# Two attentions of a second transformer block: both heads of a pair at once on TensorE's halves, the softmax factor moved behind the values, the causal mask added by a matmul

## The reference, cut to what matters

```python
def chunked_attention(q, k, v, q_gain, k_gain, rel_bias):   # called branch A here
    q = rms_norm(q, q_gain); k = rms_norm(k, k_gain)
    scores = einsum(q, k over a band of 9 chunks of 64) * (dh ** -0.5)
    scores = where(valid, scores + bias, -inf)
    probs = softmax(scores, axis=-1)
    return probs @ v

def stick_breaking_attention(q, k, v):                      # called branch B here
    z = einsum(q, k) * (dh ** -0.5)
    causal = key_pos < q_pos
    log_keep = where(causal, -softplus(z), 0.0)
    log_after = cumsum(log_keep, reverse=True) - log_keep
    w = where(causal, exp(log_sigmoid(z) + log_after), 0.0)
    return w @ v
```

## Time and profile before

| | us |
|---|---|
| median of 3 runs | 3797.51 (3796.48 to 3799.83) |
| the profiled execution: time | 3795.74 |
| the profiled execution: span | 3794.0 |
| PE busy / DVE / ACT / POOL | 3467.8 / 1802.0 / 1093.5 / 538.9 |

### The profile page before, as it was taken

One profiled execution on the slowest core, in us unless ns is written; L12 is line 12 of the kernel. 1 busy time (PEld: TensorE's weight loads), 2 busy tenths in 40 slices (PEclk: granted clock), 3 DMA queues, 4 the chain that ended last, 5 costly groups with the idle time before them and its releaser, 6 DMA issues.

```text
span 3794.0 us, 35643 instructions
## 1 busy us (share of the span) xinstructions
PE 3467.8 (91%) x14866; PEld 2670.4 (70%) x14866; DVE 1802.0 (47%) x2004; ACT 1093.5 (29%) x1540; POOL 538.9 (14%) x554
## 2 busy tenths in 40 slices
PE   6888997998788999999987999988989989999999
PEld 4567785666666888788765788744447768878887
DVE  5563446877755223322353541177773354433443
ACT  3331113552223112211241221244651122222222
POOL 2301200224421000000042000000554000000000
PEclk9889998999998999999998999989999999999999
DMA  4343442014321112211213234301103211121122
GB/s 143 123 139 133 141 142 89 20 40 136 122 95 62 55 47 76 78 50 50 77 45 145 86 104 133 95 17 34 34 17 133 89 38 48 60 89 56 45 67 100
DMA packets 86535, 308.60 MB, mean 81 GB/s; under 512 B 10311, under 2 KB 12871, under 8 KB 85992
## 3 DMA queue, kind: packets, MB, share of 16 engines
q1 hardware_dynamic: 57800, 203.04, 16.9%
q0 software_dynamic: 28576, 103.30, 7.9%
HBM read 254.92 MB, written 51.38 MB: 81 GB/s over the span
## 4 chain that ended last, share of the span: by engine, by line
PE 59%; DVE 10%; issue 5%; ACT 2%; POOL 1%; DMA 0%; DVEq 0%; ACTq 0%; POOLq 0%
PE PS L233 18%; PE PS L235 18%; PE PS L234 18%; PE PS L2251 3%; DVE st L2339 1%; DVE E L2337 1%; DVE E L2356 1%; PE PS L2219 1%; DVE tmp L1588 1%; DVE QR L1268 1%; PE PS L2233 0%; ACT WT L2301 0%; DVE hid L1932 0%; PE PS L2014 0%; DVE R L1583 0%
## 5 line engine op out<-in xcount | busy, mean ns | idle before, releaser
L233 PE MATMUL PS<-H,HL 128*128 128x512 f32 x2880 | 1145.3, 398 | 78.3 <-DVE H L441 13.4
L234 PE MATMUL PS<-H,HL 128*128 128x512 f32 x2880 | 1130.8, 393 | 0.0
L235 PE MATMUL PS<-H,HL 128*128 128x512 f32 x2880 | 1130.4, 393 | 0.0
L203 ACT ACTIVATE HL<-RAW 128x1024 fp32r<-128x1024 f32 x316 | 334.2, 1058 | 1823.6 <-PE PS L235 1705.3
L233 PEld LDWEIGHTS PS<-H,HL 128*128 128x128 f32 x2880 | 546.5, 190 | 219.6 <-issue 45.0
L235 PEld LDWEIGHTS PS<-H,HL 128*128 128x128 f32 x2880 | 546.9, 190 | 115.8
L234 PEld LDWEIGHTS PS<-H,HL 128*128 128x128 f32 x2880 | 547.6, 190 | 114.6 <-issue 3.9
L215 DVE TENSOR_TENSOR HL<-RAW,HL 128x1024 fp32r<-128x1024 f32 x316 | 411.4, 1303 | 362.2 <-ACT HL L203 343.5
L233 PE MATMUL PS<-hs,HL 128*128 128x512 f32 x704 | 279.1, 396 | 16.2 <-DVE X L1814 6.4
L235 PE MATMUL PS<-hs,HL 128*128 128x512 f32 x704 | 279.3, 397 | 0.0
L234 PE MATMUL PS<-hs,HL 128*128 128x512 f32 x704 | 277.9, 395 | 0.0
(11 more groups left out here) (318 smaller groups left out, 4170.0 us busy)
## 6 DMA issues: line engine op xcount, KB each, us to landing
RAW<-in_w_up SPq DMA_DIRECT2D x88, 512.0 KB, 3.6
RAW<-in_w_down SPq DMA_DIRECT2D x88, 512.0 KB, 3.6
RAW<-in_w_proj SPq DMA_DIRECT2D x40, 512.0 KB, 4.3
RAW<-in_w_wmodr SPq DMA_DIRECT2D x32, 512.0 KB, 4.6
RAW<-in_w_wmod SPq DMA_DIRECT2D x16, 512.0 KB, 4.2
scr_K<-ko POOLq DMA_DIRECT2D x32, 256.0 KB, 4.4
RAW<-in_w_wqkv SPq DMA_DIRECT2D x16, 512.0 KB, 5.5
RAW<-in_w_dfwd SPq DMA_DIRECT2D x16, 512.0 KB, 3.7
```

The costliest lines, as they stand in the source:

```text
L203: e.activation(k.HL[:, m % N_HL, 0, :], k.RAW[:, j % N_RAW, :], ACT.Copy).then_inc(*k.high.mark(j))
L233: e.matmul(out, lh, rh, start=first, stop=False)
L234: e.matmul(out, lh, rl, start=False, stop=False)
L235: return e.matmul(out, ll, rh, start=False, stop=last)
```

## The change

- **Units.** A unit is a pair of heads and one tile; `UNITS` takes the place of `JOBS`. Scores of both heads are issued alternately on array rows 0 to 63 and 64 to 127 (the zero padding goes, with it two memsets and one DMA of each pair's load), values alternately on array columns 0 to 63 and 64 to 127. `WT2` holds both heads. PE works two units ahead; there are still five slots, two per unit.
- **Branch A.** The factor 1/8 goes into the gain of q. The maximum comes out negated from the reduction. The row is no longer multiplied by its reciprocal: reciprocals go to `rr`, PE spreads them over a bank after the values (eight small matmuls, signal "r"), ACT copies that to `Rb2`, DVE multiplies the values by it ("o"), then high and low halves follow. All copies of transposed blocks are ACT's.
- **Branch B.** 1/8 goes into the copy of q. The mask comes as a matmul of `identr` by `maskr` (fp32r) into the scores' last 128 columns, and POOL's two selects per job go. The product of `take` and the scanned `keep` moves from DVE to POOL. Every second copy of transposed blocks in a unit is DVE's.

```diff
+UNITS = [(br, p, 4 * gr + i) for br in range(2) for p in range(4) for gr in range(2) for i in range(4)]
...
+                b, r = 2 * hh + a // 512, slice(64 * hh, 64 * hh + 64)
+                x = e.matmul(PS[:, b, 0:w], k.q2[r, pn % 2, blk(t)], k.k2[r, pn % 2, lo * 128 + a:lo * 128 + a + w],
+                             start=True, stop=br == 0 or a + w < n)
...
+                e.matmul(PS[:, b + c // 512, c % 512:c % 512 + 128], k.identr[:, :], k.maskr[:, :], start=False, stop=True).then_inc(*s.pe.mark("s", u, hh))
...
+            for hh in range(2):
+                r = slice(64 * hh, 64 * hh + 64)
+                x = e.matmul(PS[r, ob, cols], k.v2[:, pn % 2, kb, r], k.WT2[:, hh, kb, cols], start=(kb == kbs[0]), stop=(kb == kbs[-1]),
...
+                x = e.matmul(PS[64 * hh:64 * hh + 64, b, blk(i)], k.rr[:, g % 2, c:c + 1].to_broadcast([128, 64]), k.ident[:, :], start=True, stop=True,
...
+    scores(0)
+    scores(1)
+    for u in range(NU + 1):
+        if u + 2 < NU:
+            scores(u + 2)
+        if u % 4 == 0 and u:
+            values_of(u // 4 - 1)
+        if u < NU:
+            turn(u)
```

What a slot waits for, the order of DVE's queue (its last two lines hold `o_lo`), and POOL's queue:

```diff
+def slot_free(k, e, u, hh):
+    j = 2 * u + hh - NS
+    if j >= 0:
+        e.wait_ge(*k.att2.pe.at("turn", j // 2, len(k.turns_att2[j // 2]) - 1))
...
+        e.tensor_tensor(ev, k.two(2 * hh)[:, 0:n], B[:, 2 * p + hh, 640 - n:640], ALU.add).then_inc(*s.dve.mark("biased", u, hh))
+        e.wait_ge(*s.dve.at("biased", u, hh))
+        e.tensor_reduce(st[:, sl, 0:1], ev, AX.X, ALU.max, negate=True).then_inc(*s.dve.mark("max", u, hh))
...
+        if scan:
+            left(u + 1, 0)
+        if u < NU:
+            turn(u, (0, 1))
+        if scan:
+            left(u + 1, 1)
+        if u < NU:
+            turn(u, (2, 3))
+        if g >= 0:
+            br = UNITS[4 * g][0]
+            if br == 0 and u % 4 == 0:
+                scale(g)
+            if u % 4 == (1 if br == 0 else 0):
+                low(g)
...
+        if g >= 0 and u % 8 == 0 and g // 2 + 2 < 8:
+            load_pair(k, e, g // 2 + 2)
+        if u + 1 < NU and UNITS[u + 1][0] == 1:
+            n = span(1, UNITS[u + 1][2])[1]
+            for hh in range(2):
+                sl = slot(u + 1, hh)
+                tk = Sc[:, sl, 0:n]
+                e.wait_ge(*s.dve.at("left", u + 1, hh))
+                e.wait_ge(*s.act.at("take", u + 1, hh))
+                e.tensor_tensor(tk, tk, E[:, sl, 1025 - n:1025], ALU.mult).then_inc(*s.pool.mark("w", u + 1, hh))
```

More of the change, by code:

```diff
@@ L2158, in span, with slot, turn_out, turned @@
     return lo, (t + 1 - lo) * 128
+def slot(u, hh):
+    return (2 * u + hh) % NS
 def turns_att2():
[L2163 to L2167, removed]
-    return out
[L2171 to L2200, removed]
+    out, n = [], 0
+    for br, p, t in UNITS:
+        m, unit = span(br, t)[1] // 128, []
+        for c in range(0, m, 4):
+            w = min(4, m - c)
+            for heads in (((0, 1),) if w <= 2 else ((0,), (1,))):
+                unit.append((heads, c, w, 4 + n % 2, "dve" if br and len(unit) % 2 else "act"))
+                n += 1
+        out.append(unit)
+    return out
+def turn_out(k, u, x):
+    (br, p, t), (heads, c, w, b, eng) = UNITS[u], k.turns_att2[u][x]
+    lo = span(br, t)[0]
+    n = len(heads)
+    src = k.PS[:, b, 0:n * w * 128].rearrange("p (h k n) -> p h k n", h=n, k=w)
+    return k.WT2[:, heads[0]:heads[0] + n, lo + c:lo + c + w, blk(t % 4)], src
+def turned(k, u, x):
+    return (k.att2.dve if k.turns_att2[u][x][4] == "dve" else k.att2.act).at("turn", u, x)
+def values_bank2(g):
+    return 6 + g % 2
+def slot_free(k, e, u, hh):
+    j = 2 * u + hh - NS
+    if j >= 0:
+        e.wait_ge(*k.att2.pe.at("turn", j // 2, len(k.turns_att2[j // 2]) - 1))
 def pe_att2(k, e, free):
@@ L2208, in claim, with scores @@
             e.wait_ge(*x)
[L2210 to L2211 removed]
+    def scores(u):
+        br, p, t = UNITS[u]
         lo, n = span(br, t)
[L2213 to L2215 removed]
+        pn = 4 * br + p
+        e.wait_ge(*k.in_pair[pn % 2].at(pn, 2))
         for a in range(0, n, 512):
             w = min(512, n - a)
[L2218 to L2221, removed]
@@ new lines, in factors, with high @@
+    def factors(g):
+        e.wait_ge(*s.pe.at("r", g))
+        if g:
+            e.wait_ge(*s.dve.at("o_lo", g - 1))
+        e.activation(k.Rb2[:, :], PS[:, values_bank2(g + 1), :], ACT.Copy).then_inc(*s.act.mark("r", g))
+    def high(g):
+        br, p, t = UNITS[4 * g]
+        if br == 0:
+            e.wait_ge(*s.dve.at("o", g))
+            src = k.Rb2[:, :]
+        else:
+            e.wait_ge(*s.pe.at("pv", g))
+            src = PS[:, values_bank2(g), :]
+        e.activation(H[:, 0, 4 * br + p, blk(t // 4, 512)], src, ACT.Copy).then_inc(*s.act.mark("o_hi", g))
@@ new lines, in act_att2 @@
+    for hh in range(2):
+        exponents(0, hh)
+    for u in range(NU + 2):
+        g = u // 4 - 1
+        if g >= 0 and u % 4 == 1 and UNITS[4 * g][0] == 0:
+            high(g)
+        soon = u + 1 < NU and UNITS[u + 1][0] == 0
+        later = u + 2 < NU and UNITS[u + 2][0] == 1
+        if soon:
+            exponents(u + 1, 0)
+        if later:
+            exponents(u + 2, 0)
+        if u < NU:
+            turn(u, (0, 1))
+        if soon:
+            exponents(u + 1, 1)
+        if later:
+            exponents(u + 2, 1)
+        if u < NU:
+            turn(u, (2, 3))
+        if g >= 0 and u % 4 == 0:
+            (factors if UNITS[4 * g][0] == 0 else high)(g)
```

299 lines of the change are left out of this document (139 added, 160 removed).

## The result

| | before | after |
|---|---|---|
| median, same chip | 3797.22 us (3796.48 to 3799.83) | 3826.45 us (3823.73 to 3831.12) |
| ratio | | 1.0077, 95% interval 1.006 to 1.0094 |
| profiled execution: time / span | 3795.74 / 3794.0 us | 3831.12 / 3829.3 us |
| end of branch A (last low half starts) | 2658.29 | 2638.27 |
| branch B, from there to its last low half | 185.9 us | 239.0 us |

The change costs 29.2 us by the medians (7.6 us is what such a measurement can tell), 35.3 by the two profiled spans: A ends 20.0 earlier (forecast 36), B lasts 53.1 longer (forecast 33 + 5 + 12 - 3 = 47), and 2.2 lie elsewhere. The forecast was +11: the direction and the range hold, the size is short by 18.0 by the medians (3826.45 against 3808.5) and 24 by the profiled executions, 16 of it in A, 6 in B and 2 elsewhere.

A forecast was written before the change was run, and what follows sets the result against it. No engine was full; stalls at each value group, with DVE soon out of slots, were taken to bound the kernel. -36 + 33 + 5 + 12 - 3 = +11 on 3795.7, 1.8 more for the median: 3808.5 us, range 3770 to 3838.

The forecast's parts named there:

- 33 + 5 + 12 - 3: Branch B: line and holes +33, POOL's products behind load issues +5, PE clock +12, last pair without successor -3.
- Column halves run together: Value matmuls on PE: both heads side by side, 4.7 us in A's second group, 5.97 in B's.
- the forecast's rival: PE's values and factors: column halves run one after the other over 128 rows, +60, 3868 us; chance 0.07.
- A, 37.0 per pair, -36: Branch A: DVE work 26.1, idle 4.9 and 3.6, waits 2.4 per pair; -40 for four, last output 4 later.
- A not under 40: Branch A, sign of being wrong: pairs not under 40 us would mean ACT, with all copies, is late.
- the last output's way: End of branch A: the last group's output arrives about 4 us later, through factors, copy and multiplication.
- B's line and holes, 54.8 per pair, +33: Branch B: DVE scans and POOL products exclude each other, 43.0 per pair, plus holes 8.5, 2.7 and 0.6.
- products well over 2.34: Branch B, sign of being right: POOL products take well over 2.34 us wherever a DVE scan runs.
- the hole at the pair's end: Branch B: DVE idle 8.5 us per pair, since its low half stands before the third unit's scan.
- Clock, 3 per pair of B, +12: Branch B: PE left idle between wide products drops its clock, 3 us per pair taken from bounds 0 and 8.
- Faster rival, pairs of B at 49.2: Branch B: scans and products pack tightly, clock stays up, +11 for four pairs, kernel 3769 us; chance 0.25.
- Mask matmuls, ACT's copies, 0: PE's mask matmuls and two small ACT copies cost 0; if PE lacks time, 64 masks at 0.1 cost 6.

The follow-up runs named there:

- d4_fillgap: The changed kernel plus 10 unused 128x512 matmuls per pair of branch B, behind each unit's transposes into the values' idle bank: 3802.83 us, 1.0018 of before.
- e2_fill_ab: The changed kernel plus unused matmuls behind transposes in both branches, and B's product back on DVE: 3781.63 us, 0.9961 of before.
- c3_low: The changed kernel with branch B's low half one unit later in DVE's queue, as in branch A: 3836.29 us, 1.0104 of before.
- e1_fill_prod: The changed kernel plus 10 unused matmuls per pair behind B's transposes, and B's product back on DVE; none in A: 3793.48 us, 0.9990 of before.

## Why the prediction was right, and what was mis-sized

- **The direction**: A gains, B loses more, slower on the whole. Right; the forecast had 0.55 on it. It hung on the clock alone: without that term the forecast was -1.
- **Column halves run together** (values 4.7 us in A's second group, 5.97 in B's). Right at full clock: 5.81 in B (d4_fillgap) for 5.97, 4.53 in A (the change, at 2542.36) for 4.7. Serial they would have cost 39.6; the forecast's rival had 60 for it.
- **A, 37.0 per pair, -36**. The sum was right at full clock: 36.7 at 0.95 and 35.8 at 1.00. Its parts were off by a little both ways: DVE's work is 24.1 us, not 26.1. What failed is a term that isn't there: the clock was counted in B alone, and put at nothing in A without a reason. The change's A ran at 0.80, and its pairs took 41.2 and 42.3. The forecast's own sign of being wrong, A not under 40, did come; it was to mean that ACT is late, and that it does not: ACT is busy for 21.50 of 41.15 us, and the same code took 36.7 where the clock was 0.95. A smaller thing is the handover to B: the last pair of A takes 42.9 us, and 46.4 in e2_fill_ab, where the two before take 35.8. The forecast had 4 for it, the last output's way, and in e2_fill_ab it is 10.6. DVE of the changed kernel in that pair:

```profile
2620.16 0.16 DVE L2386 RECIPROCAL rr<-st 128x1 f32<-128x1 f32 x1 [4.44 <-ACT E L2303]
...
2635.89 0.69 DVE L2408 TENSOR_TENSOR Rb<-PS,Rb 128x512 f32<-128x512 f32 x1 [8.72 <-ACT Rb L2326]
```

In a pair before it (2533 to 2550) no wait for ACT is over 0.3 us, and the one at the values, for PE, is 5.07. Here DVE waits 4.44 for A's last exponent and 8.72 over the values and the factor's copy, with only B's narrow units to do meanwhile. That the change of branch is the cause is read off, not tried.
- **B's line and holes, 54.8 per pair, +33**, with loads 5. At a clock of 0.90 a pair takes 53.8, in which the loads are contained: 54.8 and 1.3 would be 56.1, 2.3 too many. The line was overstated, in part because POOL's wide product takes 2.0 us rather than 2.34 (by the same token the sign "products well over 2.34" did not come for the single ones, while two of 896 took 5.92 beside a scan); the hole at the pair's end was right in size, 8.5 against 9.18 in d4_fillgap, and wrong in its reason (c3_low).
- **Clock, 3 per pair of B, +12**. This is the term that was mis-sized. Fill matmuls give back 5.9 per pair of B, 21.5 us for the kernel (its excess over before goes from 29.2 to 7.7), and 11.9 more in A: 33.4, with fills that take PE time of their own and leave B at 0.91. Take that from the 29.2 and -4.2 is left; the forecast without its clock term was -1 (11 less 12). In the sum, then, the miss is the clock. That all else comes out right to some 3 us is partly luck, two errors that cancel: with the clock up A ends 28.3 us earlier (2629.98 in e2_fill_ab against 2658.29) where 36 was forecast, and B lasts 29.5 longer (d4_fillgap) where 33 + 5 - 3 = 35 was.
- **Faster rival, pairs of B at 49.2**: it was said to need B under 51.4. That bound has the +12 for the clock in it, which this rival denies; without it, -36 - 3 + 4 x 7.8 = -7.8, the bound is 54.3. The change itself is at 59.8; e2_fill_ab's 51.4 has the clock nearly up and the product on DVE, and comes out faster through A, whose pairs are back at full pace.
- **Mask matmuls, ACT's copies, 0**: nothing in these traces speaks against it; ACT is busy for 96 of 239 us in B. It was not tried apart.

What stays open: why a pair of B needs 51.4 us even in e2_fill_ab, where DVE works 37.1 of it (148.41 by four). The 9 us in which DVE waits for PE's value block (d4_fillgap) are seen, a way round them was not tried. Nor was a version with the zero-padded scores of before and all else of the change, which would show directly how much of the clock goes with the row halves. The transposes and the values' 64 columns are in both kernels and the scores on 64 rows only in the changed one, which speaks for them, but by argument.

## What to carry to other kernels

Running two matmuls on halves of the array gained a factor of 1.86 here (10.80 to 5.81 us), at a clock that stays; price such a change at both levels of the clock, in every stretch that it touches, and not only where PE gets a new hole. Look at PEclk per stage right after the total: here 33 us lay in that one column, more than the net loss of 29. Where PE has waiting time off the path, full-array matmuls into an idle bank paid for themselves here, but their place decides: 18 per pair, ahead of what the next engine waits for, gained nothing at the same clock at which 10 behind it gained 5.9 us.

## What the runs showed that was not expected

- A stretch of 13.17 us in which PE is recorded busy throughout, on scores of 64 rows and transposes, stood at 1.2 GHz (0.50). And one loop can stand at either level: in e1_fill_prod one pair of A ran at 0.95 and the next, the same code, at 0.76.
- PE busy for 252.72 of 264.40 us was granted 0.76, while 179.88 of 205.78 with full-array fills was granted 0.91.
- A scan on DVE waits out a product on POOL to within 0.1 us: 5.71 for two scans of 2.05, with 1.65 of a product in their way.
- The 32 records of a group's column-half values over 128 rows took 5.81 us, one head after the other 10.80, both at a granted clock of 1.00.
